# Forget gate projection: high and low weight columns in one stationary tile

## The reference

```python
def even_mixer(h, w_in, b_f, g_v, w_s, b_s, g_qn, g_kn, w_out):
    z = h @ w_in                       # (512, 1024) @ (1024, 2568)
    uv = gelu(z[..., :1024])           # u and v of the spatial gate
    ...                                # q, k, v: 512 columns each
    f_logit = z[..., o + 3 * FOX_WIDTH:] + b_f      # the last 8 columns
    log_f = jax.nn.log_sigmoid(f_logit)
    ...
    y_a = chunk_gmlp(u, v, g_v, w_s, b_s)
    y_b = forgetting_attention(q, k, vv, log_f)     # c = cumsum(log_f)
```

## Time and the profile before

| | us |
|---|---|
| median of 3 timed executions | 1914.72 |
| lowest, highest | 1914.2, 1914.88 |
| profiled execution, its own time | 1914.05 |
| span of the profiled execution | 1912.3 |
| PE busy | 1885.5 (99%) |
| VectorE busy | 960.7 (50%) |
| GpSimd busy | 914.2 (48%) |
| ScalarE busy | 688.1 (36%) |

### The profile page before, as it was taken

How to read it: one execution, slowest core, us unless ns; L and a number is a source line. 1 busy time by engine, 2 the same in 40 slices (tenths; PEclk the granted TensorE clock), 3 DMA queues, 4 the chain that set the end, 5 groups by cost and what they waited for, 6 DMA issues and landing times.

```text
span 1912.3 us, 22817 instructions
## 1 busy us (share of the span) xinstructions
PE 1885.5 (99%) x8677; PEld 1547.5 (81%) x8677; DVE 960.7 (50%) x1245; ACT 688.1 (36%) x1016; POOL 914.2 (48%) x409
## 2 busy tenths in 40 slices
PE   7999999999999999999999999999999999999999
PEld 6778888888888878778878888888888878888887
DVE  7877955444421248555664444213856484444201
ACT  4556333232222344443633232222234543232211
POOL 2564645444454444645545444445445444445442
PEclk9999999999999999999999999999999999999999
DMA  5241122322323322123232332333233223332322
GB/s 179 67 127 66 67 66 89 105 93 88 107 80 102 119 67 88 45 66 132 67 110 88 97 100 85 102 99 98 85 132 111 88 77 100 93 105 88 99 89 76
DMA packets 165175, 178.91 MB, mean 94 GB/s; under 512 B 4696, under 2 KB 152656, under 8 KB 164849
## 3 DMA queue, kind: packets, MB, share of 16 engines
q1 hardware_dynamic: 162092, 172.10, 27.9%
q10 hardware_dynamic: 3013, 5.84, 1.0%
HBM read 175.83 MB, written 2.10 MB: 93 GB/s over the span
## 4 chain that ended last, share of the span: by engine, by line
PE 91%; DVE 5%; ACT 2%; POOL 1%; issue 1%; DMA 0%; DVEq 0%; ACTq 0%; POOLq 0%
PE acc L532 28%; PE acc L534 28%; PE acc L533 28%; PE aux L609 1%; PE aux L740 1%; PE acc L740 1%; DVE a_lo L1187 1%; ACT w_hi L1885 0%; PE aux L885 0%; PE aux L532 0%; PE aux L534 0%; PE aux L533 0%; PE acc L906 0%; ACT xp L2266 0%; DVE x L1208 0%
## 5 line engine op out<-in xcount | busy, mean ns | idle before, releaser
L2353 POOL TENSOR_TENSOR w_lo<-w_raw,w_hi 128x1024 fp32r<-128x1024 f32 x322 | 795.7, 2492 | 859.5 <-ACT w_hi L1885 859.5
L532 PE MATMUL acc<-a_hi,w_hi 128*128 128x512 f32 (+1 forms) x1480 | 581.6, 393 | 2.1 <-DVE a_lo L1187 1.2
L534 PE MATMUL acc<-a_hi,w_lo 128*128 128x512 f32 (+1 forms) x1480 | 577.6, 390 | 0.0
L533 PE MATMUL acc<-a_lo,w_hi 128*128 128x512 f32 (+1 forms) x1480 | 577.3, 390 | 0.0
L1885 ACT ACTIVATE w_hi<-w_raw 128x1024 fp32r<-128x1024 f32 x324 | 324.9, 1051 | 454.1 <-PE acc L534 427.0
L532 PEld LDWEIGHTS acc<-a_hi,w_hi 128*128 128x128 f32 (+1 forms) x1480 | 277.5, 188 | 71.0 <-issue 8.2
L534 PEld LDWEIGHTS acc<-a_hi,w_lo 128*128 128x128 f32 (+1 forms) x1480 | 277.5, 187 | 58.9
L533 PEld LDWEIGHTS acc<-a_lo,w_hi 128*128 128x128 f32 (+1 forms) x1480 | 277.6, 188 | 57.7 <-issue 0.2
L532 PE MATMUL acc<-h_hi,w_hi 128*128 128x512 f32 x528 | 206.1, 390 | 0.0
L534 PE MATMUL acc<-h_hi,w_lo 128*128 128x512 f32 x528 | 205.8, 390 | 0.0
L533 PE MATMUL acc<-h_lo,w_hi 128*128 128x512 f32 x528 | 205.7, 390 | 0.0
(11 more groups left out here) (412 smaller groups left out, 2270.0 us busy)
## 6 DMA issues: line engine op xcount, KB each, us to landing
w_raw<-in_w_gate SPq DMA_DIRECT2D x22, 1024.0 KB, 5.1
w_raw<-in_w_up SPq DMA_DIRECT2D x22, 1024.0 KB, 5.1
w_raw<-in_w_down SPq DMA_DIRECT2D x16, 896.0 KB, 4.9
w_raw<-in_hy_w_in SPq DMA_DIRECT2D x12, 1024.0 KB, 5.6
w_raw<-in_ffn_w_gate SPq DMA_DIRECT2D x11, 1024.0 KB, 5.1
w_raw<-in_ffn_w_up SPq DMA_DIRECT2D x11, 1024.0 KB, 5.1
w_raw<-in_e_w_in SPq DMA_DIRECT2D x10, 1024.0 KB, 5.0
w_raw<-in_xa_wkv SPq DMA_DIRECT2D x8, 1024.0 KB, 5.1
```

The source lines that it names most:

```text
L532: nc.tensor.matmul(o, l_hi, r_hi, start=start, stop=False)
L533: nc.tensor.matmul(o, l_hi, r_lo, start=False, stop=False)
L534: return nc.tensor.matmul(o, l_lo, r_hi, start=False, stop=stop)
L2353: nc.gpsimd.tensor_tensor(w_lo[s][:, half], w_raw[s][:, half], w_hi[s][:, half].bitcast(F32), ALU.subtract)\
```

## The change

The gate's block is no longer split in the slots w_hi and w_lo. A tile of its own, w_f (128 by 8 channel tiles by 40 columns), holds the rounded weights in columns 0 to 7, zeros in 8 to 31 and the low rest in 32 to 39. One matmul with all 40 columns by a_hi gives high by high in rows 0 to 7 of the bank and low by high in rows 32 to 39; a second with columns 0 to 7 by a_lo adds high by low to rows 0 to 7. ScalarE rounds only these 64 elements for each partition; GpSimd zeroes the gap and subtracts only the 64. VectorE copies rows 32 to 39 out, adds rows 0 to 7, and multiplies by rstd in an instruction of its own.

```diff
+    w_f = put("w_f", [P, KT, 40], F32R)
...
+    GATE_BLOCK = 18 + FT + 12 + 4
...
@@ block.tensor @@
-        wh, wl = block_in(KT, 8, whole=True)
+        block_in(KT, 8, whole=True)
         bank = open_acc("f")
         open_acc("f spare")
         for k in range(KT):
-            last = exact(bank[0:8, :], wh[:, k, :], wl[:, k, :], a_hi[:, k, :], a_lo[:, k, :], k == 0, k == KT - 1)
+            if k == KT - 1:
+                nc.tensor.matmul(bank[0:8, :], w_f[:, k, 0:8], a_lo[:, k, :], start=False, stop=False)
+            last = nc.tensor.matmul(bank[0:40, :], w_f[:, k, :], a_hi[:, k, :], start=k == 0, stop=k == KT - 1)
+            if k < KT - 1:
+                nc.tensor.matmul(bank[0:8, :], w_f[:, k, 0:8], a_lo[:, k, :], start=False, stop=False)
         last.then_inc(acc_ready, 2)
@@ block.vector @@
-        ins = V.tensor_tensor(gate[:, :], f_bank[0:8, :], rstd[0:8, :], ALU.mult)
+        step(V.tensor_copy(gate[:, :], f_bank[32:40, :]))
+        ins = V.tensor_tensor(gate[:, :], f_bank[0:8, :], gate[:, :], ALU.add)
         ins.then_inc(acc_free, 2)
...
         settle()
+        step(V.tensor_tensor(gate[:, :], gate[:, :], rstd[0:8, :], ALU.mult))
         for_act(V.tensor_scalar(gate[:, :], gate[:, :], small[0:8, 0:1], None, ALU.add))
@@ block.scalar, split_next @@
-            for half in BLK_HALVES:
-                S.activation(dst[:, half], w_raw[b % 2][:, half], ACT.Copy).then_inc(w_hi_ready, 1)
+            if b == GATE_BLOCK:
+                S.activation(w_f[:, :, 0:8], w_raw[b % 2][:, 0:8 * KT].rearrange("p (k c) -> p k c", k=KT), ACT.Copy)\
+                    .then_inc(w_hi_ready, 2)
+            else:
+                for half in BLK_HALVES:
+                    S.activation(dst[:, half], w_raw[b % 2][:, half], ACT.Copy).then_inc(w_hi_ready, 1)
@@ block.gpsimd @@
-        lo_blocks(16, FOX_BLOCK - 1)
+        lo_blocks(16, GATE_BLOCK)
+        pool.wait_ge(w_hi_ready, hi_seen.next(2))
+        nc.gpsimd.memset(w_f[:, :, 8:32].bitcast(F32), 0.0)
+        nc.gpsimd.tensor_tensor(w_f[:, :, 32:40], w_raw[GATE_BLOCK % 2][:, 0:8 * KT].rearrange("p (k c) -> p k c", k=KT),
+                                w_f[:, :, 0:8].bitcast(F32), ALU.subtract).then_inc(w_lo_ready, 2)
+        lo_blocks(GATE_BLOCK + 1, FOX_BLOCK - 1)
```

## The result

| | before | after |
|---|---|---|
| median of timed executions, us | 1914.05 (6 runs) | 1921.53 (6 runs) |
| lowest, highest | 1913.59, 1914.88 | 1920.81, 1921.73 |
| span of the profiled execution | 1912.3 | 1919.5 |

The kernel became slower: ratio 1.0037, 95% interval 1.0027 to 1.0048. The forecast was 1917.5 in a range of 1914.1 to 1918.8, so the time lies outside it, 2.7 us above its upper end. Of the cases in the text it is nearest to rival 3 (tie (a) is lost, 1919.3), with 2.2 us on top. The forecast stood on a median of before of 1914.72 from three executions, and six give 1914.05. So the loss is 7.5 us where rival 3 had 4.6, and for the other 2.9 no case had a price.

What follows compares the result with a forecast made beforehand. PE, busy 99% of the span, was taken as the bound: -1.84 (matmuls) + 1.18 + 0.55 (waits) + 0.00 = -0.11, then + 2.87 (wait at the q_raw transposes) = +2.76, giving 1917.5 us, range 1914.1 to 1918.8.

Steps and rivals of the forecast that it cites:

- rival 3: GpSimd holds the gate's bias from 714.70 to 717.4; q_raw comes 4.6 us late, 1919.3 us; chance 0.12.
- tie (a): VectorE's gate bias against GpSimd's block 58 at 714.70: VectorE is 0.08 to 0.14 us ahead and wins.
- Part 1: Gate block on PE: eight matmuls fewer at 0.230 us each save 1.84 us.
- Part 2: PE behind the gate block: waits for block 57's pieces and g_tok's scaling leave 0.11 us of gain.
- Part 3: Rounding and halving only the gate's columns on ScalarE and GpSimd: taken as 0 us for the span.
- Part 4: Three VectorE gate steps for one: 1.42 to 1.46 us more before the bias, costing nothing by busy time.
- Part 5 (b): VectorE's one-element instruction under GpSimd's block 58 piece: 0.15 us, or held to about 717.3.
- Part 5 (c): First ye_lo against GpSimd's block 59: GpSimd wins, q_raw transposes' load 2.8 us late, 1917.5 us; chance 0.55.
- The clock: Closing caveat: the prediction is wrong too if PE's idle lowers the granted clock; no size given.

Runs made afterwards that it cites:

- a3: Kernel before with one VectorE step more: a copy of rows 0 to 7 out of the bank, then the product with rstd; 1914.40 us, ratio 1.0000.
- a8: Changed kernel with the signal that frees the two banks moved from VectorE's sum to its product; 1920.18 us (one run).
- a9: Changed kernel with one more VectorE instruction, a memset of an unused column about 50 us earlier; 1920.70 us (one run).
- a1: Changed kernel with VectorE's single product as before, rows 32 to 39 not added; sixteen matmuls and small rounding stay; 1914.64 us, ratio 1.0000.
- a6: Changed kernel with the bias moved: ScalarE adds it inside its absolute value, VectorE only after the spatial gates; 1918.43 us, ratio 1.0021.
- a2: Kernel before, 24 matmuls, with three VectorE steps for one: copy, maximum with that copy, product; 1920.37 us, ratio 1.0032.
- a5: Changed kernel with 19 matmuls of 512 columns, result overwritten, in PE's wait before the q_raw transposes; 1919.33 us, ratio 1.0024.
- a7: Changed kernel with the late bias of a6, and g's inverse roots keeping their half and intermediate t in spare PSUM; 1913.54 us, ratio 0.9995.
- b2: The kernel of a7 run again on another chip, against the kernel before; 1913.85 us, ratio 0.9997.

## Why the prediction was wrong

**Part 1, right.** Sixteen gate matmuls, (706.38 - 702.92) / 15 = 0.231 each, where 0.230 was taken.

**Part 2, right in its waits, at its lower bound in the sum.** The two waits for block 57 are there: PE at 706.78 and 709.11 (forecast 706.7 and 709.1). At the spatial products 0.11 us was to be kept, bounds 0 and 0.22; it is 0 (11.02 against 11.04, the trace's own scatter). ScalarE ends at 711.23 + 2.45 = 713.68 in both kernels and PE's load is at 713.90 in both: what looked like room was the time of the release.

**Part 3, right.** ScalarE's 64 elements take 0.26 us, GpSimd's memset and subtraction 0.26 and 0.32, all before 693.2, and block 57 starts at 704.31 (before 704.29).

**Part 4, the step that failed.** "Two more cost 1.42 to 1.46 us; the bias starts at 714.56 to 714.62 ..." Each step is indeed 0.71 (a3), but the three together start the bias at 715.14. Over the forecast's middle that is 0.55 more, which two pieces make up: 0.12 since the copy from rows 32 to 39 doesn't overlap the g_tok product, and 0.45 (0.48 less the usual 0.03) in front of the sum. Neither had a row before. The part held its sum to be free because idle time of 0.87 and 1.80 lay behind it, and took the two extra steps from the nearest row with no upper bound beyond 0.04 of spread.

**Part 5 (a), so lost.** The prediction named 0.1 us as the point from which rival 3 decides and gave it a chance of 0.12. The excess was five times that; in a8 and a9, with an excess of only 0.15 counted from the first gate matmul, the bias was 0.06 to 0.07 behind and lost as well. The Trainium skill (SBUF — State Buffer, section Who interferes with whom) says that issue order decides who blocks; the trace agrees, 714.70 against 715.14 and a bias of 2.46. The working of rival 3 was right in size: bias to 717.4 (717.6), decays from 722.0 (722.27), ye_lo pair to 731.8 (732.2), q_raw at 749.1 (749.3), PE 4.6 late (4.5 at the first transpose).

**Part 5 (b), settled.** L1607 is not held: 0.15 at 718.18, under GpSimd's second piece, and 0.15 in a3. The Trainium skill (VectorE: DVE Perf Modes, section What auto-detection actually checks) gives a condition that one element doesn't meet; the runs agree.

**Part 5 (c), not reached, but its price was right.** With PE gaining nothing, GpSimd came at 724.45 as before and met the decays. In a1 VectorE was 0.07 ahead and won; in a6 it was 0.01 behind and lost, at +2.79 on the load against the 2.8 worked out. The forecast of 1917.5 needed GpSimd 0.11 earlier at (c), or L1607 held, and had neither. So had the bias won as forecast, a1 and a3 speak for a time like that of before and not for 1917.5. That the kernel became slower at all, as forecast, is luck: it did so by tie (a), which the prediction held to be won.

**The clock, named and not priced.** "if PE's idle lowers the granted clock" stood in the last paragraph without a number. It is 2.65 us of the 7.16. On the median of before from six executions, 1914.05 + 4.6 (rival 3) + 2.65 = 1921.3, beside the measured 1921.53. It belonged into every case with a wait at the transposes, (c) too (a6: 1.46).

## What to carry to other kernels

An edit that adds short steps on an engine sharing a port is to be priced by where each step starts against the other engine's next instruction, not by the idle time behind it; if the margin is a tenth of a microsecond, treat the tie as open and price both outcomes. A wait of TensorE like the ones here (2.4 to 4.4 us) costs itself and the slow work behind it (1.2 to 2.65 us). And work removed from the engine that is busy 99% can be worth nothing, as in a1, until the appointments behind it move too; find these first.

## What was not expected of the hardware

- A sum that waits for the step ahead and signals PE started 0.48 us after it instead of 0.03 in a2, a5, a6, a7, b2 and after. With the signal moved it was 0.03, with one unrelated memset ahead 0.11.
- After 4.37 us of idle PE ran at granted clock 0.50 for 6 us (transposes 3.67 us for 1.91), and after 2.43 us too (3.38 us). In a8 and a9, after 4.10 us, the part behind the wait was only 1.2 and 1.5 us. The price follows how much work ran at 0.50 and not the length of the wait: 6.0 us of it cost 2.65 (after), 5.0 cost 2.1 (a2), 3.4 cost 1.5 (a6, a9), 2.9 cost 1.2 (a8). In a6 and a9 the clock fell only once PE was back at work. Waits of PE of 1.4 us elsewhere in before (at 222.4 us, for one) left it at 1.00.
- A long wait isn't all that brings the lower clock. In the traces of a5 and a9 it was 0.50 for 3.3 us from 176 us on too, and in the 26 us ahead PE was busy but for one wait of 0.42. That lies ahead of this stage and isn't in the columns above.
- A copy from rows 32 to 39 of PSUM starts 0.11 later, relative to the product ahead of it, than one from rows 0 to 7 (after against a2; a1, with the matmuls of after and a read of rows 0 to 7, starts as early as a2).
- GpSimd against VectorE for the port: VectorE 0.07 ahead wins (a1), 0.01 behind loses (a6). The one behind waited out the other's whole instruction.
